# Attention in a two-layer decoder block: the odd head's probabilities scaled by GpSimd, the second branch's turned weights copied by VectorE

## What is computed

```
p_c = masked_softmax(sc, cmp_end[None, :] <= tq[:, None])
o_c = jnp.einsum('bgrqn,bgnd->bqgrd', p_c, v_cmp)
...
p_s = masked_softmax(ss, m_s)                 # selected blocks
o_s = jnp.einsum('bgrqkl,bgqkld->bqgrd', p_s, vs)
...
o_w = jnp.einsum('bgrqk,bgkd->bqgrd', masked_softmax(sw, m_w), vw)   # window
return gb[..., 0:1] * o_c + gb[..., 1:2] * o_s + gb[..., 2:3] * o_w
```

## Time and profile before

| | |
|---|---|
| three runs | 947.06, 947.16, 948.44 us; median 947.16 us |
| the profiled execution, its own time | 948.35 us |
| its span (first to last instruction) | 946.6 us |
| granted TensorE clock, mean | 0.999 of full speed |
| start of the exponentials X(2), X(5), X(6), X(7) | 655.12, 676.89, 683.72, 690.56 us from the span's start |
| first matmul of "wo" | 695.70 us |

### The profile page before, as it was taken

The page is one execution under the profiler, slowest core; times in us unless marked ns, Lnnn a source line. Parts: engine busy times, 40 slices in busy tenths (PEclk is TensorE's granted clock), DMA queues, the critical chain, the costliest instruction groups (busy, mean ns, idle before and its releaser), DMA issues.

```text
span 946.6 us, 14028 instructions
## 1 busy us (share of the span) xinstructions
PE 899.7 (95%) x5289; PEld 759.1 (80%) x5289; DVE 587.9 (62%) x980; ACT 523.2 (55%) x931; POOL 23.8 (3%) x46
## 2 busy tenths in 40 slices
PE   6999989899999999999999899998889999999998
PEld 5889978787888877888888788897567788888876
DVE  5767984758676575555544666767757555554465
ACT  6644756676766465444444548446866544444452
POOL 6000000000000000000000000000000000000000
PEclk9999999999999999999999999999999999999999
DMA  9941201111113556677645554520025555655552
GB/s 343 329 135 45 90 28 62 45 46 45 46 46 136 184 170 221 224 231 255 196 159 195 182 201 134 179 89 2 1 90 178 177 179 179 189 191 173 183 187 97
DMA packets 105898, 138.28 MB, mean 146 GB/s; under 512 B 4585, under 2 KB 76786, under 8 KB 105842
## 3 DMA queue, kind: packets, MB, share of 16 engines
q1 hardware_dynamic: 103650, 130.15, 42.5%
q0 software_dynamic: 2160, 7.36, 2.0%
q10 hardware_dynamic: 32, 0.01, 0.0%
HBM read 136.45 MB, written 1.05 MB: 145 GB/s over the span
## 4 chain that ended last, share of the span: by engine, by line
PE 74%; DVE 11%; ACT 11%; issue 2%; DMA 1%; SPq 0%; ACTq 0%; DVEq 0%
PE ps L504 16%; PE ps L506 16%; PE ps L505 16%; PE ps L483 4%; PE ps L488 4%; DVE w_lo L1587 4%; PE ps L489 4%; PE ps L490 4%; ACT w_hi L1115 3%; PE ps L736 3%; PE ps L718 2%; DVE gdn L1654 1%; PE ps L1001 1%; ACT qkvT L1521 1%; DVE gdn L1789 1%
## 5 line engine op out<-in xcount | busy, mean ns | idle before, releaser
L1587 DVE TENSOR_TENSOR w_lo<-w_raw,w_hi 128x2048 fp32r<-128x2048 f32 (+2 forms) x100 | 220.7, 2207 | 199.4 <-ACT w_hi L1115 199.3
L1115 ACT ACTIVATE w_hi<-w_raw 128x2048 fp32r<-128x2048 f32 (+2 forms) x100 | 184.5, 1845 | 185.6 <-PE ps L506 140.4
L504 PE MATMUL ps<-w_hi,x_hi 128*128 128x512 f32 x480 | 193.5, 403 | 11.5 <-DVE gdn L1820 5.7
L506 PE MATMUL ps<-w_hi,x_lo 128*128 128x512 f32 x480 | 187.6, 391 | 0.0
L505 PE MATMUL ps<-w_lo,x_hi 128*128 128x512 f32 x480 | 187.2, 390 | 0.0
L504 PEld LDWEIGHTS ps<-w_hi,x_hi 128*128 128x128 f32 x480 | 90.2, 188 | 34.5 <-DVE gdn L1820 7.5
L506 PEld LDWEIGHTS ps<-w_hi,x_lo 128*128 128x128 f32 x480 | 90.1, 188 | 19.4
L505 PEld LDWEIGHTS ps<-w_lo,x_hi 128*128 128x128 f32 x480 | 90.4, 188 | 16.6
L488 PE MATMUL ps<-x_hi,w_hi 128*128 128x256 f32 x320 | 92.0, 287 | 0.9 <-DVE w_lo L1587 0.6
L489 PE MATMUL ps<-x_lo,w_hi 128*128 128x256 f32 x320 | 90.5, 283 | 0.0
L490 PE MATMUL ps<-x_hi,w_lo 128*128 128x256 f32 x320 | 90.5, 283 | 0.0
(11 more groups left out here) (311 smaller groups left out, 1478.8 us busy)
## 6 DMA issues: line engine op xcount, KB each, us to landing
w_raw<-in_ffn_w_in SPq DMA_DIRECT2D x88, 512.0 KB, 4.6
w_raw<-in_ffn_w_out SPq DMA_DIRECT2D x40, 512.0 KB, 4.2
w_raw<-in_gdn_w_in SPq DMA_DIRECT2D x28, 512.0 KB, 4.7
gdn<-in_gdn_w_in SPq DMA_DIRECT2D x20, 512.0 KB, 7.3
w_raw<-in_gdn_w_out SPq DMA_DIRECT2D x16, 512.0 KB, 4.2
w_raw<-in_ple_w_gate SPq DMA_DIRECT2D x16, 512.0 KB, 4.5
w_raw<-in_kv_w SPq DMA_DIRECT2D x12, 512.0 KB, 4.2
qkvT<-in_cmp_w POOLq DMA_DIRECT2D x8, 512.0 KB, 5.0
```

Source lines behind the costliest of these rows:

```text
L504: mm(o, hi, w_h, start=first and kk == 0, stop=False, skip_group_check=True)
L506: return mm(o, lo, w_h, start=False, stop=end and kk == n - 1, skip_group_check=True)
L1115: A(whi[:, place(stage, q), c0:c0 + n], ring_raw(u) if stage == "qkv" else raw[:, q, 0:n], ACT.Copy).then_inc(S["hi_done"], 1)
L1587: V.tensor_tensor(wlo[:, s, c0:c0 + n], ring_raw(u) if stage == "qkv" else raw[:, q, 0:n], whi[:, s, c0:c0 + n], ALU.subtract).then_inc(S[ ...
```

## The change

GpSimd gets 32 new instructions, four for each pair, that scale the odd head's probabilities; VectorE still makes the reciprocal and the gate product for the odd head, and no longer scales it. ScalarE copies only the first branch's turned weights; VectorE copies the second branch's (two copies per pair, new function `turned_out`). On VectorE `weights(p, 1)` now stands directly behind `weights(p, 0)`, ahead of the maxima of the short scores. `pts_act` counts half as many copies as before, `pts_dve` and `pw_pool` are new, and the semaphore `conv_extra` of layer 0 is merged into `conv_dve`, with the waits counted accordingly.

```
@@ gpsimd, behind its last transfer
+            for p_ in range(8):
+                pool.wait_ge(S["rl_dve"], 4 * p_ + 4)
+                for b in range(2):
+                    par = p_ % 2
+                    w = hst[:, 2 * par + 1, 2, :]
+                    g.tensor_scalar(pr0[:, par, 1, b, :], pr0[:, par, 1, b, :], w[:, b:b + 1], None, ALU.mult)
+                    g.tensor_scalar(pr1[:, par, 1, b, :], pr1[:, par, 1, b, :], w[:, 2 + b:3 + b], None,
+                                    ALU.mult).then_inc(S["pw_pool"], 1)
@@ tensor: turned(p, e), output(p), and p == 3
-                    pe.wait_ge(S["pw_dve"], 4 * p + 2 * e + b + 1)
+                    pe.wait_ge(S["pw_pool" if e else "pw_dve"], 2 * p + b + 1)
                     if p or e:
-                        pe.wait_ge(S["pts_act"], 4 * p + 2 * e + b - 1)
+                        pe.wait_ge(S["pts_dve" if b else "pts_act"], 2 * p + e)
...
-                pe.wait_ge(S["pts_act"], 4 * p + 4)
+                pe.wait_ge(S["pts_act"], 2 * p + 2)
+                pe.wait_ge(S["pts_dve"], 2 * p + 2)
...
-                    pe.wait_ge(S["pts_act"], 16)
+                    pe.wait_ge(S["pts_dve"], 8)
@@ scalar: turned(p, e)
-                for b in range(2):
-                    act.wait_ge(S["ptr_ps"], 4 * p + 2 * e + b + 1)
-                    A(pts[:, p % 2, e, b], bank(6 + b, 3, P), ACT.Copy).then_inc(S["pts_act"], 1)
+                act.wait_ge(S["ptr_ps"], 4 * p + 2 * e + 1)
+                A(pts[:, p % 2, e, 0], bank(6, 3, P), ACT.Copy).then_inc(S["pts_act"], 1)
@@ vector: conv(u)
-                            dve.wait_ge(S["conv_dve"], n0 + 2 * (m - 1) + n + 1)
+                            dve.wait_ge(S["conv_dve"], 5 * u + 2 * (m - 1) + n + 1)
...
-                                S["conv_done"] if (j, n) == (0, 1) else S["conv_extra"] if j == 0 else S["conv_dve"], 1)
+                                S["conv_done"] if (j, n) == (0, 1) else S["conv_dve"], 1)
@@ vector: weights(p, e) and the order of the pairs
+                if e:
+                    return
...
+            def turned_out(p, e):
+                if p >= 2:
+                    dve.wait_ge(S["av_ps"], p - 1)
+                dve.wait_ge(S["ptr_ps"], 4 * p + 2 * e + 2)
+                V.tensor_copy(pts[:, p % 2, e, 1], bank(7, 3, P)).then_inc(S["pts_dve"], 1)
...
             weights(0, 1)
             q_out(2)
+            turned_out(0, 0)
+            turned_out(0, 1)
...
                 weights(p, 0)
+                weights(p, 1)
                 if p < 7:
                     maxima(p + 1, 0, 0)
                     maxima(p + 1, 1, 0)
-                weights(p, 1)
+                turned_out(p, 0)
                 if p < 7:
                     maxima(p + 1, 0, 1)
                     maxima(p + 1, 1, 1)
+                turned_out(p, 1)
```

More of the change, by code:

```diff
@@ L243, in build @@
                      "res_ps res_sb ss_b fin_ps tr_ps ht_ps g_ps ple_m kv_ps v_sb kv_sb q_sb tk_ps tk_sb ba_ps ba_dve ba_act "
-                     "tap_done conv_dve conv_extra conv_done silu_done l2_sq sum_ps sum_sb sumt_ps l2_dve l2_root cum_ps cum_act cum_dve "
+                     "tap_done conv_dve conv_done silu_done l2_sq sum_ps sum_sb sumt_ps l2_dve l2_root cum_ps cum_act cum_dve "
                      "gtri_done kq_ps dA_ps dA_ex dQ_ps dQ_ex qs_ps qs_sb a_sb qk_sb kt_ps ktok_sb vt_ps bv_sb w_init "
@@ L248, in build @@
                      "sg_done hid_done fhi_done flo_done pt_ps phi_done plo_done sgm_done "
-                     "ablk_act ablk_dve pts_act w1_in hid_ps hb_sb hid_sb kc_ps kc_sb "
+                     "ablk_act ablk_dve pts_act pts_dve pw_pool w1_in hid_ps hb_sb hid_sb kc_ps kc_sb "
                      "gt_ps gt_dve gt_done cs_ps cs_dve cs_act pct_ps pct_sb fx_dve "
```

## The result

The changed kernel took 959.31 us (median of four runs, 956.53 to 963.01), the kernel before, run beside it, 947.8. The ratio is 1.0125, 95% interval 1.0108 to 1.0141: **slower** by 1.25%, clear of the noise, by over 11 us in the median, and outside the predicted range of 946.2 to 951.2. The profiled execution took 956.53 us with a span of 954.8, 8.2 more than the profiled one before.

A forecast was written before the change was run, and what follows sets the result against it. TensorE waits about 1 us of each 6.83 us lap, on a chain through ScalarE's copies; 0.86 lost at the start, 0.56 won between and 0.86 lost at the end take the median 947.16 to 948.3 us, range 946.2 to 951.2.

The forecast's parts named there:

- GpSimd's scalings: Odd head's scalings on GpSimd, priced from its selects: 0.36 us for 128 columns, 0.50 for 256, 0.86 a branch.
- P: GpSimd's time for the four odd-head scalings of a pair: 1.72 us, bounds 1.2 and 2.88 (four times 0.72).
- the forecast's own sign of being wrong: Laps below 6.4 us, TensorE waiting for GpSimd inside plain laps, or a difference arising outside the attention.
- Pair 0: First pair: TensorE stands still for GpSimd before the last transposes, query unit behind them later, +0.86 us.
- Pair 1: Second pair: GpSimd ends at 650.72, T1's second branch due at 650.73; no loss, but no room left.
- ScalarE's route: Lap bound by ScalarE's copies: one copy of T1 fewer, 0.37 us less, 6.46 instead of 6.83.
- VectorE's route: Lap through S1, its maxima, VectorE's copy, O, S0 and T0: 6.65 us, a gain of 0.18.
- The two laps of GpSimd: From X(p) through factors, GpSimd, copy and O to X(p+2): 10.84 + P, 6.28 us a lap, hidden up to P = 2.4.
- X(3) to X(4): Lap between exponential starts of pairs 3 and 4: `cmp_turned` waits for VectorE's copy, X(4) +1.03 us against before.
- the rival of a slow GpSimd: Scalings cost by columns: +2.5 us at P = 2.16, +5.7 at P = 2.88; chance 0.28, at some 949.8 us.
- Pair 7: Last pair: nothing covers GpSimd between its factors and "wo"; 0.86 us lost at the end.
- the +1.16: Total displacement of "wo" in us: 0.86 lost at the start, 0.56 won between, 0.86 lost at the end.

The follow-up runs named there:

- free_scaling: The change without GpSimd's four odd-head scalings per pair, those probabilities left unscaled: 947.38 us, ratio 1.0002.
- pool_narrow: The change with GpSimd's second scaling of a branch on 128 of 256 columns, the others left unscaled: 953.69 us, ratio 1.0063.
- widths: The kernel before plus a series on GpSimd after the attention (scalings of 32 to 512 columns, a copy) that nothing waits for; attention stretch 71.23 us.
- again: The changed kernel measured once more, no edit, beside the other experiments: 957.85 us, ratio 1.011 to the kernel before.
- weighted_first: The change with VectorE's `cmp_weighted` of the second half moved ahead of its copy of T1(2): 961.62 us, ratio 1.0139.

## Why the prediction was wrong, step by step

**GpSimd's scalings: the step that failed.** It read "For 128 columns I take 0.36", and for 256 "I take 0.50". Measured are 0.60 and 0.90 from start to start, P = 3.0 for 1.72. With it came the forecast's own sign of being wrong, waits of TensorE for GpSimd inside plain laps (0.89 us at 682.18). The rows it came from are masks by `TENSOR_SCALAR_AFFINE_SELECT`, which do 128 columns in 0.29 to 0.30. A select is no guide to a multiplication: from 16 to 256 columns a scaling's duration rises by some 2.5 ns a column (328, 602, 921 ns for 16, 128, 256), on top of about 0.29 us; the selects' slope was 0.6. The bounds were at fault too: "four times 0.72" took the dearest row at hand for an upper end, and nothing in it was a multiplication. An estimate from the Trainium skill, "GPSIMD Engine Reference", section "Performance versus the Vector engine", was 1.5 ns a column; the prediction set it aside as a neighbour of a rival, and these runs show it nearer than the selects and still too low. (It is 2.5 times the selects' slope, not three times.)

**Pair 0: right mechanism, P off.** Its own formula gives +0.86 at P = 1.72 and so +2.14 at P = 3.0; counted from the start of the stretch, the query unit began 18.03 us in, before 15.97: +2.06. Pair 1, "nothing, but with no room left", comes by the same arithmetic to 650.72 + 1.28 - 650.73 = 1.27, and X(1) to X(2) is 1.27 longer than in `free_scaling`. The two formulas make 3.41 at P = 3.0. X(0) to X(2) is 3.32 longer than before, where 0.86 was forecast; 3.11 of it is GpSimd's by `free_scaling`, and the other 0.21 has no term in the forecast.

**ScalarE's route: right.** 6.46 forecast, 6.46 and 6.43 measured where it binds.

**VectorE's route: right, 0.14 short.** 6.65 forecast, 6.79 measured without scaling. O took 1.88 for 1.78, and the copy with the start of O 0.65 for 0.61 (the copy itself 0.55, forecast 0.56). S1 to its maxima looks 0.08 longer and S0 to T0 0.06 shorter only because the forecast took the starts of S1 and T0 from the chain (681.11, 680.30), and the timeline before has them at 681.04 and 680.23. The "gain" of 0.18 a lap became 0.04.

**The two laps of GpSimd: right.** 10.84 + 3.0 = 13.84; X(4) to X(6) took 14.02. (The terms named add up to 10.79; 10.84 holds the second handover of 0.05, from VectorE to GpSimd, which the list leaves out.) "Hidden, up to P = 2.4" agrees with `pool_narrow`, where X(5) to X(7) is only 0.14 above `free_scaling`.

**X(3) to X(4): missed.** Forecast 8.70, without scaling 8.96, in the change 10.70; the rival of a slow GpSimd had only +0.5 for `cmp_turned` there. The timeline of VectorE, GpSimd and TensorE in this lap:

```profile
663.71 1.29 DVE L2115 TENSOR_REDUCE head_stats<-ps 128x2 f32<-128x512 f32 x2 [0.53 <-PE ps L1013]
665.71 0.56 DVE L2174 COPY qkvT<-ps 128x384 f32<-128x384 f32 x1 [0.71 <-PE ps L491]
666.18 0.39 DVE L2140 TENSOR_REDUCE cmp_stats<-gdn 128x16 f32<-128x240 f32 x1
```
```profile
664.08 0.92 POOL L482 TENSOR_SCALAR qkvT<-qkvT,head_stats 128x256 f32<-128x256 f32 x1
669.88 0.60 POOL L481 TENSOR_SCALAR qkvT<-qkvT,head_stats 128x128 f32<-128x128 f32 x1 [4.89 <-DVE head_stats L2159]
```
```profile
665.05 0.55 PE L491 MATMUL ps<-ident,qkvT 128*128 128x128 f32 x3 [0.90 <-POOL qkvT L482]
```

VectorE's copy waits for T1(2), T1(2) for GpSimd; `cmp_weighted` and pair 3's factors stand behind that copy in VectorE's queue; and on those factors GpSimd waits. So P counts twice in this lap: `pool_narrow`, with 0.6 less, has it 1.28 shorter, and from X(2) to X(3), in the same two profiles, nothing changed (6.46 and 6.44). That a copy which waits holds up what is queued behind it was asked of ScalarE's queue, not of VectorE's.

**Pair 7: right mechanism.** Its own share of the +1.16 is 0.86 at P = 1.72, which is 2.14 at P = 3.0. Against X(7), `wo` moved by 2.04.

**The clock: not foreseen.** No step had a lower clock for the work behind a wait. In the second profile of the change it cost 1.46 and about 1.3 us at two places, of the size by which the medians (+10.3 and +11.5) lie above the +8.2 of the first; in the runs without a profile it can't be placed, so for that part of the loss the clock is argued and not shown.

**The rival of a slow GpSimd** was the one that came true, but its +5.7 at P = 2.88 was 2.5 short of the profiled +8.2. X(3) to X(4) alone is 2.0 of it: 8.16 and 0.5 there, 10.70 measured. With P = 3.0 the same terms give about 6 us (2.14 + 1.27 + 0.5 + 2.14), and the forecast would have been "slower" without a doubt. Even P = 1.8 costs 1.7 us in the stretch, and `free_scaling` shows that with GpSimd's time at nothing the plan gains 0.1 there.

## What to carry to other kernels

Price an operation on an engine from a row of the same operation, and where there is none, let the upper bound leave the rows of other operations; then compute at that bound, not at the middle, whether the change can still pay. Before work is moved to another engine, ask what the kernel would gain if that engine took no time at all: here 0.1 us in the stretch and nothing in the median, so no price could have made it good. A copy that waits for a slow engine delays all that is queued behind it, so look for the factor or maximum behind it on which that slow engine itself waits.

## What the runs showed of the hardware

A scaling of GpSimd that begins while VectorE runs an instruction with two inputs in SBUF stands still until that one ends. In `widths`, VectorE's and GpSimd's rows:

```profile
753.42 2.29 DVE L1604 TENSOR_TENSOR w_lo<-w_raw,w_hi 128x2048 fp32r<-128x2048 f32 x1 [2.72 <-ACT w_hi L1132]
```
```profile
753.53 3.62 POOL L484 TENSOR_SCALAR qkvT<-qkvT,eps_cols 128x512 f32<-128x512 f32 x1
```

At 2.5 ns a column and 0.29, 512 columns alone are about 1.6 us (an estimate from the widths above); 3.62 less 1.6 is 2.0, nearly the 2.2 that the subtraction still ran. One of the two scalings of 128 columns, begun 0.26 into another such subtraction, took 2.56 and the other 0.60. A scaling of 32 columns that was under way when that subtraction began took 0.35, as the other of that width (0.37). The Trainium skill, "SBUF — State Buffer", section "Who interferes with whom", has this rule, with the shared ports going to whichever of the two issues first, and by these rows the trace agrees. In the attention of the change no such instruction of VectorE fell beside a scaling: the 16 scalings of each width lie within 593 to 608 and 912 to 923 ns.

TensorE's granted clock fell from 2.4 to 1.2 GHz in some runs behind its waits for GpSimd and not in others with the same waits. In `again`, the work behind it cost 1.46 us more before X(2) and about 1.3 after the start of `wo`; in `weighted_first` O(2) took 1.42 more, and with two falls its X(0) to X(2) was 4.7 longer than in a profile of the change without any.
